# Two chained transformer blocks: modulation sums moved and regrouped, the embedding gate's follow-up work lagged, weighted squares on ScalarE, an early table load

## The reference, cut to what matters

```python
ff = jnp.square(jax.nn.relu(jnp.einsum('bsd,df->bsf', hn, w_ff1[i])))
h = h + jnp.einsum('bsf,fd->bsd', ff, w_ff2[i])
hg = rms_norm(h, norm3_g[i])
ple_gate = jax.nn.sigmoid(jnp.einsum('bsd,de->bse', hg, w_ple_gate[i]) + b_ple_gate[i])
h = h + ple_gate * jnp.einsum('bsq,qd->bsd', p[i], w_ple[i])
x = rms_norm(h, final_g)
...
mod = jnp.dot(jax.nn.silu(c), ada_w[l]) + ada_b[l]
sh1, sc1, g1, sh2, sc2, g2 = jnp.split(mod, N_MOD, axis=-1)
h = rms_norm_2(x, norm1_g[l]) * (1 + sc1) + sh1
z = jnp.einsum('bsd,de->bse', h, w_in[l]) + b_in[l]
```

## Time and profile before

| | us |
|---|---|
| median of 3 runs | 957.74 |
| lowest and highest | 956.72, 959.43 |
| the profiled execution | 960.41 |
| its span, first to last instruction | 958.8 |
| TensorE busy in it | 920.3 |
| VectorE busy | 734.6 |
| ScalarE busy | 564.0 |

### The profile page before, as it was taken

The page is one execution under the profiler, slowest core; times in us unless marked ns, Lnnn a source line. Parts: engine busy times, 40 slices in busy tenths (PEclk is TensorE's granted clock), DMA queues, the critical chain, the costliest instruction groups (busy, mean ns, idle before and its releaser), DMA issues.

```text
span 958.8 us, 18424 instructions
## 1 busy us (share of the span) xinstructions
PE 920.3 (96%) x7352; PEld 891.1 (93%) x7352; DVE 734.6 (77%) x1157; ACT 564.0 (59%) x810; POOL 1.9 (0%) x9
## 2 busy tenths in 40 slices
PE   7999999999999999999999699999899989999995
PEld 5999989999999999999999688899899989999995
DVE  6778889978758799898888799977658785555453
ACT  6848366665676767644436478577675564444442
POOL 0000000000000000000000000000000000000000
PEclk9999899999999999999999899999999999999998
DMA  8656435545455799999863355444345546655541
GB/s 322 221 191 222 154 123 166 167 161 176 156 178 173 263 342 359 362 336 348 310 224 111 110 179 184 138 155 157 104 144 183 178 161 191 190 188 192 181 131 44
DMA packets 52532, 188.77 MB, mean 197 GB/s; under 512 B 5968, under 2 KB 6240, under 8 KB 52320
## 3 DMA queue, kind: packets, MB, share of 16 engines
q1 hardware_dynamic: 52160, 187.34, 57.5%
q10 hardware_dynamic: 288, 0.27, 0.1%
HBM read 186.53 MB, written 1.05 MB: 196 GB/s over the span
## 4 chain that ended last, share of the span: by engine, by line
PE 76%; DVE 14%; ACT 7%; issue 3%; DMA 0%; DVEq 0%; ACTq 0%
PE bank L952 22%; PE bank L955 22%; PE bank L954 22%; DVE wlo L986 4%; ACT whi L1751 2%; PE bank L928 1%; PE bank L927 1%; PE bank L926 1%; DVE mqk L1328 1%; DVE cv L1060 1%; PE bank L665 1%; DVE t L1028 1%; DVE nrm L1001 1%; ACT P L1862 1%; DVE Alo L1021 1%
## 5 line engine op out<-in xcount | busy, mean ns | idle before, releaser
L986 DVE TENSOR_TENSOR wlo<-raw,whi 128x1024 fp32r<-128x1024 f32 x297 | 360.7, 1222 | 107.7 <-ACT whi L1751 107.1
L1751 ACT ACTIVATE whi<-raw 128x1024 fp32r<-128x1024 f32 x297 | 311.1, 1055 | 215.2 <-PE bank L955 199.7
L952 PE MATMUL bank<-Alo,whi 128*128 128x256 f32 x1376 | 391.2, 284 | 6.4 <-DVE wlo L986 3.3
L954 PE MATMUL bank<-Ahi,wlo 128*128 128x256 f32 x1376 | 385.5, 280 | 0.0
L955 PE MATMUL bank<-Ahi,whi 128*128 128x256 f32 x1376 | 385.0, 280 | 0.0
L952 PEld LDWEIGHTS bank<-Alo,whi 128*128 128x128 f32 x1376 | 260.0, 189 | 12.1 <-issue 8.5
L954 PEld LDWEIGHTS bank<-Ahi,wlo 128*128 128x128 f32 x1376 | 260.1, 189 | 0.6 <-issue 0.2
L955 PEld LDWEIGHTS bank<-Ahi,whi 128*128 128x128 f32 x1376 | 259.9, 189 | 0.0
L955 PE MATMUL bank<-Fhi,whi 128*128 128x256 f32 (+1 forms) x288 | 82.0, 285 | 0.0
L954 PE MATMUL bank<-Fhi,wlo 128*128 128x256 f32 (+1 forms) x288 | 81.3, 282 | 0.0
L952 PE MATMUL bank<-Flo,whi 128*128 128x256 f32 x256 | 72.5, 283 | 0.0
(11 more groups left out here) (388 smaller groups left out, 1363.2 us busy)
## 6 DMA issues: line engine op xcount, KB each, us to landing
raw<-in_stream SPq DMA_DIRECT2D x297, 512.0 KB, 4.1
araw<-in_ada SPq DMA_DIRECT2D x48, 512.0 KB, 6.1
TB<-in_TB SPq DMA_DIRECT2D x1, 1536.0 KB, 7.1
out<-H SPq DMA_DIRECT2D x4, 256.0 KB, 2.2
bc<-in_bc SPq DMA_DIRECT2D x1, 896.0 KB, 5.6
H<-in_xT SPq DMA_DIRECT2D x3, 256.0 KB, 6.2
raw<-in_stream SPq DMA_DIRECT2D x2, 256.0 KB, 4.8
mats<-in_mats SPq DMA_DIRECT2D x1, 449.0 KB, 8.9
```

The costliest lines, as they stand in the source:

```text
L952: pe.matmul(os[j], wh, xl, start=k == 0 and (wide or j == 0), stop=False, skip_group_check=not wide)
L954: pe.matmul(os[j], wl, xh, start=False, stop=False, skip_group_check=not wide)
L986: v.tensor_tensor(wlo[:, s % NHL, :], raw[:, s % NRAW, :], whi[:, s % NHL, :].bitcast(F32), ALU.subtract).then_inc(*lo_v.up(s))
L1751: a.activation(whi[:, s % NHL, :], raw[:, s % NRAW, :], ACT.Copy).then_inc(*hi.up(s))
```

## The change

Six things change.
1. **Modulation sums.** The 48 products are ordered block by block: all eight of one column block, then the next. Only two accumulators of 1024 columns are left (`aacc0`, `aacc1`, used in turn). The first eight products stand at slabs 66 to 81, the other 40 at slabs 97 to 147, 1.3 slabs apart. A block's eight transposes stand two slabs behind its last product (slabs 83, 108, 118, 128, 139, 149) and its two reductions one slab further, in PSUM banks 6 and 7. Gains and shifts are made at slab 152. SyncE now steps on its own list.
2. **The gate's follow-up.** Per pair, VectorE drains first and makes a slab's low part between the drain and the wait for the sigmoid; ScalarE makes the high part behind the sigmoid. `ahead` and the weighted squares leave `after_pair` and become the task `emb`, at slabs 165, 167, 169 and at the end of the fourth pair.
3. **Weighted squares.** ScalarE makes them in one go: Square with `g2` as scale, `g2` being now the square root of what it was (a root at slab 98). VectorE only adds 512 columns per pair, and TensorE sums the two halves (two matmuls in place of one).
4. **Plain squares** for `final` are made at slabs 175 to 181 (task `A`), with the column total at 183, again two matmuls, root at 184, reciprocal at 186. The scalings of `H` move to slabs 187 to 192.
5. **Tables.** At the start ScalarE runs one Copy on a spare column ahead of its first wait, and one Sqrt on it behind the fourth pair of the gate.
6. **Start.** The second x transfer moves from ScalarE's queue to SyncE's, behind the first half of slab 0. The silu of c is made at slab 58.

```diff
-AFTER_VECTOR = ("br3", "wo", "ff2", "pg", "pm", "wo2", "dn") + ...
+AFTER_VECTOR = ("br3", "wo", "ff2", "pm", "wo2", "dn") + ...
...
+ADA = [66, 68, 70, 72, 74, 77, 79, 81] + [97 + i * 13 // 10 for i in range(40)]
+SUMS = [ADA[8 * b + 7] + 2 for b in range(6)]
...
-    "trig": [98, 100, 102, 104, 106, 108],
-    "ada": [97 + b + b // 4 for b in range(48)] + [157, 158, 159, 160, 160.5, 161, 161.5],
-    "r2": [98, 99, 100],
+    "trig": ([], [98, 100, 102, 104, 106, 108], [104, 110]),
+    "ada": ([], ADA, [58]),
+    "sums": (SUMS, [n + 1 for n in SUMS] + [SUMS[5] + 3], []),
+    "r2": ([98], [96, 100, 101], [98]),
     "xb": [172, 173, 174, 174],
-    "final": [179, 182, 185, 188, 191],
+    "emb": ([], [165, 167, 169], [165, 167, 169]),
+    "A": ([183], [177, 178, 181, 186], [175, 178, 180, 184]),
+    "final": ([], [187, 188, 190, 192], []),
...
                     if n >= 3:
                         w.wait_ge(*ada_v.at(n - 3))
+                    else:
+                        w.wait_ge(*gla_s.at("hi", 3))
+                        w.wait_ge(*gla_v.at("lo", 3))
+                        w.wait_ge(*gla_pe.at("o", 1))
...
+                if q == 0:
+                    load_x(1)
...
+            def sums():
+                for cb in range(6):
+                    w.wait_ge(*mats_in.at("in"))
+                    w.wait_ge(*ada_v.at(8 * cb + 7))
+                    if cb:
+                        w.wait_ge(*red_v.at(cb - 1))
+                    else:
+                        w.wait_ge(*att_s.at("p", 3, 1))
+                    for j in range(8):
+                        i = pe.transpose(banks[6 + j // 4][:, j % 4 * 128:j % 4 * 128 + 128],
+                                         aacc[cb % 2][:, j * 128:j * 128 + 128], ident)
...
-                        pe.matmul(banks[6][:, 0:T], ones[:, :], aw, start=True, stop=True).then_inc(*aw_pe.up("aw"))
-                        total("A", 7)
+                        for j in range(2):
+                            i = pe.matmul(banks[6][:, 0:T], ones[:, :], aw2[:, half(j)], start=j == 0, stop=j == 1)
...
             def weighted(p):
-                w.wait_ge(*sq.at("A", p))
-                ...
-                add_squares("A", p, t)
+                if p:
+                    w.wait_ge(*sq.at("aw", p))
...
+                    v.tensor_tensor(aw2, araw[:, 0, 512:1024] if p == 1 else aw2, araw[:, p % 2, 512:1024], ALU.add
+                                    ).then_inc(*aw_v.up(p))
...
                     i.then_inc(*drained_v.up((name, p)))
+                    low_part(ENDS[name, p] + 3)
                     w.wait_ge(*emb_s.at("pg", p))
...
-                    ahead("pg", p, lambda k: modg[:, k:k + 1], hib, lob)
-                    if p:
-                        weighted(p - 1)
+                    if p == 3:
+                        next(tasks["emb"])
...
-                        if (name, n) in ENDS and ENDS[name, n] >= 1:
+                        if (name, n) in ENDS and ENDS[name, n] >= 1 and name != "pg":
                             low_part(ENDS[name, n] + 3)
...
+            def emb():
+                for p in range(4):
+                    ahead("pg", p, lambda k: modg[:, k:k + 1], hib)
...
+                    for j in range(2):
+                        i = a.activation(araw[:, p % 2, 512 + j * T:512 + (j + 1) * T], H[:, 2 * p + j, :], ACT.Square,
+                                         scale=g2[:, 2 * p + j:2 * p + j + 1])
+                    i.then_inc(*sq.up("aw", p))
+                    yield
...
+            def normed():
+                w.wait_ge(*xb_v.at(7))
+                square("A", 0, t512[0][:, :])
+                square("A", 1, t512[1][:, :])
+                yield
+                for p in (2, 3):
+                    w.wait_ge(*added.at("A", p - 1))
+                    square("A", p, t512[1][:, :])
+                    yield
...
-                    ahead("pg", p, lambda k: modg[:, k:k + 1], hib)
-                    if p >= 2:
-                        w.wait_ge(*added.at("A", p - 2))
-                    square("A", p, araw[:, p % 2, 512:1024])
+                    high_part(ENDS[name, p] + 4)
+                    if p == 3:
+                        next(tasks["emb"])
+
+                        a.activation(spare, ones[:, 0:1], ACT.Sqrt)
...
-            a.dma_start(H[:, 2:4, :], A["xT"][:, 2:4, :]).then_inc(*x_in[1].up("in", by=16))
+
+            w.wait_ge(*ones_v.at("set"))
+            a.activation(spare, ones[:, 0:1], ACT.Copy)
```

More of the change, by code:

```diff
@@ L77 @@
 UNNORMED = ("v", "gv", "gk")
-AFTER_VECTOR = ("br3", "wo", "ff2", "pg", "pm", "wo2", "dn") + tuple(f"zu{j}" for j in range(1, NF2 // 2))
+AFTER_VECTOR = ("br3", "wo", "ff2", "pm", "wo2", "dn") + tuple(f"zu{j}" for j in range(1, NF2 // 2))
 ASIDE = {("gv", 1): 4}
@@ L248, in build @@
     pe_steps, v_steps, s_steps = steps
+    sp_steps = {}
+    for n in ADA:
+        sp_steps.setdefault(n, []).append("ada")
     with ctx:
@@ L331, in build @@
         ang, kf, pT = ple[:, 2, :], ple[:, 3, :], ple[:, 4:6, :]
-        g2 = modg[:, 16:24]
+        g2, csil = modg[:, 16:24], shb
+        aacc = (aacc0, aacc1)
+        aw2 = nrm[:, 0:2 * T]
         xb_ = Fhi[:, :, :].rearrange("p a t -> p (a t)")[:, 0:16 * (T + 2)].rearrange("p (h k t) -> p h k t", h=2, k=8)
@@ L501, in sync_program @@
                             load_slab(int(s))
-                    for task in v_steps.get(n, ()):
+                    for task in sp_steps.get(n, ()):
                         if task in tasks:
@@ L653, in att @@
                     yield
-            def ada():
-                for _ in range(48):
-                    yield
[L658 to L668, removed]
+            def sums():
[9 more added lines that the diff above has]
+                                         aacc[cb % 2][:, j * 128:j * 128 + 128], ident)
+                    i.then_inc(*ada_pe.up(cb))
+                    yield
             def r2():
                 total("r2", 3)
+                yield
+            def normed():
+                w.wait_ge(*added.at("A", 3))
+                for j in range(2):
+                    i = pe.matmul(banks[7][:, 0:T], ones[:, :], t512[0][:, half(j)], start=j == 0, stop=j == 1)
+                i.then_inc(*summed.up("A"))
                 yield
@@ L941, in tensor_program @@
                         os = [b[:, 0:T + 2], banks[second][:, 0:T + 2]]
-                        w.wait_ge(*(ada_v.at("red", 11) if name == "mq0" else ml_s.at("root", 1, 1)))
+                        w.wait_ge(*(red_v.at(5) if name == "mq0" else ml_s.at("root", 1, 1)))
                         if name == "zu0":
@@ L1261, in ada @@
                 w.wait_ge(*ada_s.at("c"))
[L1262 to L1266, removed]
-                        v.tensor_scalar(o, araw[:, i, :], csil[:, k:k + 1], None, ALU.mult).then_inc(*ada_v.up(n))
-                    else:
-                        w.wait_ge(*ada_v.at(n - 6))
-                        v.scalar_tensor_tensor(out=o, in0=araw[:, i, :], scalar=csil[:, k:k + 1], in1=o,
-                                               op0=ALU.mult, op1=ALU.add).then_inc(*ada_v.up(n))
-                    yield
@@ L1280, in ada, with sums @@
+            def sums():
+                for cb in range(6):
+                    w.wait_ge(*ada_pe.at(cb))
+                    for j in range(2):
+                        i = v.tensor_reduce(mod[:, 8 * cb + 4 * j:8 * cb + 4 * j + 4],
+                                            banks[6 + j][:, :].rearrange("p (a c) -> p a c", a=4), AXX, ALU.add)
+                    i.then_inc(*red_v.up(cb))
+                    yield
+                w.wait_ge(*red_v.at(5))
                 v.tensor_tensor(mod[:, :], mod[:, :], cols[:, COFF["adab"]:COFF["adab"] + 48], ALU.add
@@ L1313, in final @@
                         yield
+            def emb():
+                for p in range(4):
+                    ahead("pg", p, lambda k: modg[:, k:k + 1], hib, lob)
+                    weighted(p)
+                    yield
             def mconv():
```

106 lines of the change are left out of this document (61 added, 45 removed).

## The result

The changed kernel takes 946.89 us, the median of 4 runs (944.66 to 948.18); the kernel before took 957.23 us beside it. The ratio is 0.9887, 95% interval 0.9859 to 0.9915: 10.8 us less, give or take 2.7. I had said 947.9 us. The profiled execution took 944.66 us, 943.4 us of it span.

What follows compares the result with a forecast made beforehand. TensorE, busy 96% of the span, leaves only gaps, mostly in the gate, where VectorE is the bound. Terms -0.9 - 0.3 - 9.1 + 0.5 = -9.8 us: 950.6 profiled, 947.9 us median; range 944.3 to 952.8 us.

Steps and rivals of the forecast that it cites:

- Start: Kernel start: table load hidden in ScalarE's wait, first half slab landing somewhat earlier; -0.9 us, between 0.3 and 1.28 won.
- Sums from slab 66: Eight products moved to slabs 66 to 81: about 0, bounds 0 and +1.5 us, first one idle 2 to 4 us.
- The 48 transposes: Still 48; two blocks in the short "ple" stage each lose some 0.15 us: -0.3 us.
- Gate stage: Embedding's gate, pg: VectorE's new order per pair brings the second norm's reciprocal 9.1 us sooner: -9.1 us.
- Behind it: Slabs 175 to 187: moved plain squares and more column totals bring the diagonal later: +0.5 us, bounds 0 and +3.
- (1): Given back behind the gate: VectorE and ScalarE wait for each other at slabs 178 and 181; +4.5 us, 952.4; chance 0.17.
- (2): Slower: all eight early products wait for their transfers, TensorE waits 14.9 us; 962.8 us; chance 0.04.
- (3): The lag does not hold: ScalarE's queue in the gate as slow as VectorE's was, 8.6 us a pair; 956.5; chance 0.05.
- (4): More: whole 1.28 us at the start, squares cost 0.6, diagonal's 0.91 us wait goes; -12.5 us, 945.2; chance 0.10.

Runs made afterwards that it cites:

- run 6: Changed kernel with the second pair of x columns fetched over ScalarE's queue again, table still loaded early: 947.92 us, ratio 0.9904.
- run 3: Changed kernel with VectorE again putting the weights on the squares, plain squares of the other norm staying behind the gate: 946.92 us, ratio 0.9893.
- run 4: Changed kernel without the one-column root that loads the root's table early: 944.97 us, ratio 0.9873.
- run 12: Kernel of run 10 with the spare tile nine columns wide instead of one: 942.08 us, ratio 0.9834.
- run 5: Changed kernel without ScalarE's one-column copy at the start, so its table loads once the first data are in: 944.14 us, ratio 0.9878.
- run 7: Changed kernel with the 48 products at their old slabs, 97 to 155, still summed block by block: 948.93 us, ratio 0.9913.
- run 9: Kernel before with only one unused one-column tile allocated ahead of the stages' tiles, no instruction changed: 955.54 us, ratio 0.9973.
- run 1: Changed kernel with pg's slab halves back behind everything and the embedding's step made for each pair at once: 953.62 us, ratio 0.996.
- run 2: Kernel before with only the lag added in the gate; VectorE still weights and sums the squares: 950.13 us, ratio 0.9929.
- run 8: Changed kernel with the plain norm's root moved to step 187, reciprocal to 209, scalings of H to 210 to 216: 942.31 us, ratio 0.9849.
- run 10: As run 8, with ScalarE's slab copy ahead of the early table load and the first Silu one step later: 942.04 us, ratio 0.9839.
- run 11: Kernel of run 10 with the spare tile two columns wide instead of one: 941.24 us, ratio 0.9828.

## Why the prediction was right

*Start, predicted -0.9, measured -1.5 at the first matmul and -2.2 at the 9th slab half.* The mechanism was right, the size off: this term was too small by 0.6 to 1.3 us. I held the half slab's landing, 5.7 to 6.0 us, for the bound, and the moved transfer for "somewhat earlier": it made the half slab at least 1.4 us earlier (run 6), and that is what let the hidden load count. Beyond it, TensorE's slow beginning (matmuls of 512 columns take 0.63 us there, 0.39 us later) ended at 8.9 us instead of 12.2; in runs 3, 4 and 12, which start at 5.5 us too, it ended at 11.2 to 11.7, and the 9th half came only 1.0 to 1.2 us earlier. So the start is worth 1.0 to 2.2 us. The Trainium skill, "ScalarE: Activation LUTs", What ACT_TABLE_LOAD costs, would have made the load alone worth up to 2.66 us; run 5 puts its removal at 1.16 us, and neither of the two loads has a drain beside its 1.28 us.

*Sums from slab 66, predicted about 0.* The first product waited 1.64 us (I said 2 to 4), the other seven not, and TensorE had no new wait up to slab 97, as forecast. What I missed is that the early start is needed: I held that the 4.07 us idle at slab 97 falls away and gives nothing, but in the block order a wait of that kind helps to put VectorE behind. TensorE then waits 2.0 us, and the stretch up to P is 2.8 us longer (run 7). As a term against the kernel before it stays near 0. The 48 transposes won 0.3 us, as predicted, but not where I had put it. From the start of the matmul ahead of a block to the start of the one behind it, five of the six blocks of the kernel before take 0.91 us and the last takes 1.24; in the changed kernel all six take 0.91. I had taken 0.15 us from each of two blocks. The place of tiles has no share in this: the last block takes 1.25 us in run 9 as well.

*Gate stage, predicted -9.1, measured -9.4.* First drain 6.2 us behind pg's first matmul (I had 6.7), periods 5.4, 6.2, 5.8 (5.3, 5.9, 5.9), tail 8.6 (8.6). Runs 1 and 2 show why: periods from the lag, tail from the squares' part. My chain for the tail held: load, one-column root, slab copy, VectorE's slab half and the reciprocal follow each other without a gap from 534.10 to 537.72 us. It doesn't tell what the early load is worth, though: without it the stretch is only 0.3 us longer (run 4), since the load delays the copy behind it. What ScalarE's weights were worth, 0.1 us, I never separated.

*Behind it, predicted +0.5, measured +2.1.* This step failed in size. The idle time at slab 178 was 1.83 us (1.9), but I treated the path to the diagonal as a sum of VectorE's work and left out what stood directly ahead of it: ScalarE's root and its table load at step 184, which delay a slab copy (VectorE idle 1.45 us for it), and the reciprocal, which still stood ahead of the diagonal, 1.74 us in slab 186. The diagonal waits 1.4 us instead of 0.91, and ScalarE, with two squares (1.1 us) more ahead of the first Silu's table load, drains mq1 so late that TensorE waits another 0.8. Runs 8 and 10 remove the first and then the second: 1.9 and 1.0 us. The column total at slab 183 takes another 0.9 us of TensorE's time, which makes up the rest; that is read from the trace and was not run alone. I had held that the 0.5 us covers the column totals.

*Not in the prediction at all: -2.5 us* by the place of tiles (run 9). The misses have both signs: about 1.3 us at the start, 0.3 in the gate and 2.5 here were won beyond the forecast, and 1.6 us behind the gate were lost, so 2.5 us too little gain was forecast. The profiled pair has another 3.2 us by chance. The medians, with an uncertainty of 2.7 us, show neither. That the forecast median lies within 1.0 us of the measured one is therefore partly luck; what the runs bear out is the gate, nine tenths of the forecast.

*Rivals.* (1), given back behind the gate, is partly what happened: 2.1 us of its 5. (2) and (3) are out: one of the eight early products waited, and the lag holds, with drains at most 6.2 us apart. (4) held for the start and not for the rest: the gate gave 9.4 and not 10.5 us, and the diagonal's wait grew.

## What to carry to other kernels

Where an engine is the bound of a stage and the weight copies stand last in its queue, put them in the hops where it waits for the other engine; this took 6.5 of the 9.4 us. A step that is moved out of a tight stage has to be placed by what stands directly behind it in the queue: the norm's tail ahead of the diagonal cost 1.9 us, and moving its reciprocal 23 slabs later won them again. An accumulation that begins with a wait for its first transfer should begin where the engine has slack. Price terms of a microsecond by stretches between marks of the trace; medians of a few runs move by more than that with the granted clock.

## What the runs showed of the hardware

- The place of tiles in SBUF changes how densely matmuls run. Start to start, the three forms that read Y tiles average 120.0 ns in the kernel before and 118.6 with one unused one-column tile more ahead of them; those that read A tiles, allocated ahead of that place, 116.8 to 117.1 ns in all runs. It is worth some 2.5 us here. Which property of the address counts stays open: two columns changed nothing, nine moved the M and U tiles to 117.3 and left the Y tiles. Place is not all: in 800 to 880 us, at a granted clock of 1.00, the matmuls on A tiles start 117.8 ns apart in runs 2, 7, 10 and 11 and 116.7 ns apart in the other ten profiles (680 matmuls of all kinds in that window in run 10, 686 in run 8), though the tiles of runs 7, 8 and 10 lie in the same places. That is 1 us more from 760 to 930 us, and its cause is open.
- TensorE's granted clock fell to half at 112 to 124 us, with no wait over 0.15 us in the 25 us ahead of it, in 6 of 14 profiled executions and in both kinds of kernel. What starts it is open.
- At the start TensorE leaves its slow rate (matmuls of 512 columns in 0.63 us, then 0.39) 3.5 to 6.1 us after its first matmul (14 profiled executions), and the same start does not give the same end: 8.9, 9.8 and 11.5 us for starts at 5.45 to 5.46 us.
